# Openings that end job by job, gates that open by halves, and a gate chain woven into the splits of a ten-stage float32 kernel

## The chip, the cores and the metric

The kernel runs on one core of a Trainium2 chip. The metric is the device time in microseconds of one execution; lower is better. The engines are called PE (TensorE), DVE (VectorE, "the vector engine"), ACT (ScalarE), POOL (GpSimd) and SP (SyncE, which here only issues DMAs). Each engine runs its own list of instructions in order and they meet in semaphores.

## The reference, cut to what matters

One sequence of 512 positions and 1024 features goes through two blocks in float32. The first has four layers (a gated convolution, "fox" attention with forget gates, a gated delta rule "gdn", and sliding window attention "swa"), each as x = x + mixer(rms_norm(x)). The second has two layers, each a mixer ("hg", then latent attention "mla"), a squared-relu MLP and a gated embedding ("ple"), with a norm behind each:

```python
for i in range(2):
    a = rms_norm_2(h, pre_mix_norm[i])
    m = hgrn2_mixer(a, ...) if i % 2 == 0 else mla_mixer(a, positions, ...)
    h = h + rms_norm_2(m, post_mix_norm[i])
    f = squared_relu_mlp(rms_norm_2(h, pre_mlp_norm[i]), w_mlp_in[i], w_mlp_out[i])
    h = h + rms_norm_2(f, post_mlp_norm[i])
    e = p[i] @ w_ple_proj[i]
    g = sigmoid(h @ w_ple_gate[i])
    h = h + rms_norm_2(g * e, ple_norm[i])
```

In the fox layer a small projection gives one forget logit a head: log_f = log_sigmoid(f_logit + b_f), c = cumsum(log_f), and the scores get c_i - c_j. In mla the rotary part of queries and key is turned by cos and sin of positions times inverse frequencies.

## The kernel before, in words

All activations are kept transposed: 8 tiles of 128 features by 512 positions. Everything that is multiplied is split into a high part (rounded to the fast float32 format, fp32r) and a low part (the rest), and each product is three matmuls: high x high, low x high, high x low (L1269 to L1271; L421 to L423 for the products of `product`). The work of PE is a list of **jobs**. A job is one block of weights, 8 tiles of 128 x 128 for 128 output features, and so 24 matmuls into one PSUM bank. Jobs go through four slots (`SLOTS`) in turn: slot, bank and buffers are the job's number modulo 4. SP loads the raw weights of a job (L284), ACT writes their high part (`weight_high`, L355, 128 x 1024, for the job three or four ahead, and only when the job that had the slot is done), POOL writes the low part in two halves (L371), PE waits for the first half at the job's start and for the second at its fifth tile (`job_parts`). ACT's `weight_high` calls are written by hand between its other work, so POOL's work and PE's jobs hang on ACT's order.

Activations are split the same way: ACT writes the high part, DVE the low part, and PE waits tile by tile (`split_wait`).

**Statistics.** For an rms norm the squares of the 8 tiles are added up in `root` by DVE (L545, L755). PE multiplies the sum with a matrix of ones (L489 in `stat_tensor`, L627 in `stat_sum`), ACT takes Ln and Exp (L504, L506, `root_scalar`) and so gets `rstd`. `preload_act_table_set` makes ACT load its function table at that place (ACT_TABLE_LOAD); other loads are put in by the compiler where a function of another set follows.

`stat_tensor` stands at the end of hg, ple0, mla and ple1. It puts three matmuls of the identity with a matrix of ones (`keep_busy`, L478, float32, result unused) before the statistics matmul and eight behind it.

**Raw openings.** After the norm the next stage starts on unscaled activations. `raw_quad` runs the first four jobs of mlp0, mlp1, mla and of both ple gates together, tile by tile: for each of tiles 0 to 6 three matmuls of each of the four jobs, then the last tile of each job; in mlp and mla the statistics matmul comes after the second of these. In mlp the norm's `rstd` is applied behind the job (L2777 on DVE: relu and scale), then ACT squares (L2738) and copies (L2740), and only then comes the `weight_high` of job 4, which PE needs next. `raw_opening` does the like for fox, gdn, swa and hg.

**ple.** `ple_pe` first runs two projection jobs (their slots are those of gate jobs 2 and 3), then `raw_quad` over gate jobs 0 to 3, then jobs 4 to 7. `ple_act` takes out the projections, splits (`post_act`), and issues `weight_high` for gate jobs 2 and 3 after its steps k = 3 and k = 6 of 8. Then for each gate job n it waits for the job, issues the `weight_high` of job n + 4, takes the sigmoid out of the bank (L2892) and squares the product of the job before. In ple0 it also issues the DMA of the positions before this loop, and `rope_sines` (L1931, L1932) after job 5. `ple_dve` multiplies gate and embedding (L2919), adds squares, and in ple0 does two steps of `rope_angles` (L1904 to L1917, 15 instructions, each waiting for the one before) after each gate product.

**fox.** `raw_opening` runs jobs fox_f (gate logits) and c0 (q of head 0), `opening` jobs c0+1 and c0+2 (k and v) as the normed splits fox_h arrive, then PE waits for the copy of v, transposes it (L1040) and goes into head 0. ACT does all eight splits, then Exp and Ln of the gate chain (L1088, L1090), three weight copies, and then the loop over heads (L1097: copies of q, k, v). DVE does all of `renorm_vector`, then the gate chain (L1133 to L1148), one after the other.

**mla.** Five input jobs and a key job, norms of the query and key latents (`mla_q`, `mla_kv`), then four rope jobs, each giving two products (bank of the job, and one bank "second" that all four share, claimed anew by each). ACT copies both out (L3127, L3129), PE multiplies each with the rotation matrix (L3009), DVE turns it (L3219, L3220, L3222). ACT does the whole kv norm before the first of these copies. Then come the head pairs; their first scores are L3067.

## Time and profile before

| what | before |
|---|---|
| median of 3 runs | 2883.2 us (2882.43 to 2883.86) |
| profiled execution | 2881.76 us, span 2879.9 us |
| PE busy | 2720.0 us (94%) |
| DVE, ACT, POOL busy | 48%, 42%, 37% |
| matmuls | 13740 |
| mean granted clock of PE | 0.984 |

Times in rows are microseconds from the start of the span. PE's matmuls are pipelined: a 128 x 512 matmul is recorded as 0.39 us and the next starts 0.23 us after it, so the distance of starts is what counts. A granted clock of 1.00 is 2.4 GHz, of 0.50 is 1.2 GHz.

### The profile page before, as it was taken

To read this page: it belongs to the slowest core of one execution; us is meant where nothing else is said; L and a number is where in the kernel's file an instruction comes from. 1 tells how busy PE (TensorE), PEld (TensorE's weight loads), DVE (VectorE), ACT (ScalarE), POOL (GpSimd) and SP (SyncE) were. 2 spreads that over 40 slices of the span, in tenths; PEclk is the share of its full clock that TensorE was granted. 3 is DMA by queue.
4 is the path that set the end of the run, shared out by engine and by line. 5 is a ranking of instruction groups with operands and counts; after the bars stand their busy time and mean duration, and the time that the engine had idled before them with its cause. 6 is when DMAs were issued, how large, how long until landed. Compare 5 with 4: busy or idle time off the path is not lost.

```text
span 2879.9 us, 41743 instructions
## 1 busy us (share of the span) xinstructions
PE 2720.0 (94%) x13740; PEld 2142.4 (74%) x13740; DVE 1384.1 (48%) x2462; ACT 1212.5 (42%) x1881; POOL 1072.0 (37%) x803
## 2 busy tenths in 40 slices
PE   7999999899999899999999999988899999999997
PEld 6887777667676677778887888876667767788875
DVE  6335333776767567577655112246653444222134
ACT  4224433544443545465544233334453453333242
POOL 5454333422322332344343444433412213444442
PEclk9999999999999999999999999999999999999999
DMA  4322222211111221222222333321201102333331
GB/s 165 95 88 83 70 73 66 74 52 44 46 41 48 61 74 59 74 73 75 71 81 62 107 98 99 99 80 59 81 30 49 53 29 66 93 97 94 95 95 44
DMA packets 59639, 211.84 MB, mean 74 GB/s; under 512 B 6688, under 2 KB 7072, under 8 KB 59552
## 3 DMA queue, kind: packets, MB, share of 16 engines
q1 hardware_dynamic: 57744, 206.89, 23.4%
q10 hardware_dynamic: 1520, 2.75, 0.3%
q8 instruction: 53, 0.87, 0.1%
q0 software_dynamic: 288, 1.05, 0.1%
q14 instruction: 34, 0.28, 0.0%
HBM read 208.57 MB, written 2.10 MB: 73 GB/s over the span
## 4 chain that ended last, share of the span: by engine, by line
issue 46%; PE 24%; POOL 22%; DVE 7%; ACT 1%; POOLq 0%; DMA 0%; DVEq 0%; SPq 0%; ACTq 0%
POOL weights_low L371 22%; PE bank L1269 7%; PE bank L1271 6%; PE bank L1270 6%; DVE work L1705 2%; PE bank L1372 1%; PE bank L1050 1%; PE bank L1070 1%; DVE work L1702 0%; DVE work L954 0%; DVE work L952 0%; PE bank L1354 0%; PE bank L1059 0%; DVE activations_low L451 0%; DMA weights_raw<-weights 0%
## 5 line engine op out<-in xcount | busy, mean ns | idle before, releaser
L371 POOL TENSOR_TENSOR weights_low<-weights_raw,weights_high 128x512 fp32r<-128x512 f32 x776 | 1043.2, 1367 | 1659.0 <-ACT weights_high L355 1641.3
L1269 PE MATMUL bank<-activations_high,weights_high 128*128 128x512 f32 x2912 | 1189.9, 409 | 57.4 <-POOL weights_low L371 39.8
L1271 PE MATMUL bank<-activations_high,weights_low 128*128 128x512 f32 x2912 | 1144.2, 393 | 0.0
L1270 PE MATMUL bank<-activations_low,weights_high 128*128 128x512 f32 x2912 | 1142.9, 392 | 0.0
L1269 PEld LDWEIGHTS bank<-activations_high,weights_high 128*128 128x128 f32 x2912 | 552.4, 190 | 195.7 <-POOL weights_low L371 40.3
L1271 PEld LDWEIGHTS bank<-activations_high,weights_low 128*128 128x128 f32 x2912 | 551.0, 189 | 117.8
L1270 PEld LDWEIGHTS bank<-activations_low,weights_high 128*128 128x128 f32 x2912 | 553.1, 190 | 111.6 <-issue 9.6
L355 ACT ACTIVATE weights_high<-weights_raw 128x1024 fp32r<-128x1024 f32 x384 | 403.7, 1053 | 336.6 <-PE bank L1271 329.4
L2791 DVE TENSOR_TENSOR mixed<-bank,mixed 128x512 f32 (+1 forms) x48 | 33.2, 692 | 193.9 <-PE bank L1271 193.9
L2777 DVE SCALAR_TENSOR_TENSOR work<-bank,rstd 128x512 f32<-128x512 f32 x64 | 44.2, 691 | 158.9 <-PE bank L1271 144.2
L2738 ACT ACTIVATE to_split<-work 128x512 f32<-128x512 f32 x64 | 40.5, 632 | 189.4 <-DVE work L2777 189.4
L2782 DVE TENSOR_TENSOR activations_low<-to_split,activations_high 128x512 f32 x64 | 46.1, 721 | 104.5 <-ACT activations_high L2740 104.5
L1705 DVE SCALAR_TENSOR_TENSOR work<-work 128x512 f32<-128x512 f32 x72 | 81.0, 1125 | 2.0
L421 PE MATMUL bank<-activations_high,weights_high 128*128 128x512 f32 x168 | 73.2, 436 | 8.6 <-DVE activations_low L451 3.0
L1372 PEld LDWEIGHTS bank<-work 64*64 64x64 f32 x1344 | 47.7, 134 | 38.6 <-issue 38.6
L423 PE MATMUL bank<-activations_high,weights_low 128*128 128x512 f32 x168 | 66.8, 397 | 0.0
L1372 PE MATMUL bank<-work 64*64 64x64 f32 x1344 | 58.3, 223 | 8.8 <-DVE work L1813 7.8
L422 PE MATMUL bank<-activations_low,weights_high 128*128 128x512 f32 x168 | 66.5, 396 | 0.0
L3261 DVE TENSOR_REDUCE sink_rows<-bank 128x1 f32<-128x512 f32 x64 | 44.1, 688 | 34.7 <-PE bank L3071 34.7
L755 DVE TENSOR_TENSOR root<-root,squares 128x512 f32<-128x512 f32 x48 | 42.9, 895 | 35.4 <-ACT squares L746 34.9
L1590 ACT ACTIVATE work<-bank 128x256 f32<-128x256 f32 x40 | 15.5, 387 | 104.2 <-PE bank L1372 104.2
L3091 PE MATMUL bank<-work 128*128 128x512 f32 x128 | 56.8, 597 | 1.3 <-ACT work L3169 1.3
(438 smaller groups left out, 3151.2 us busy)
## 6 DMA issues: line engine op xcount, KB each, us to landing
weights_raw<-weights SPq DMA_DIRECT2D x388, 512.0 KB, 3.6
out_t<-residual SPq DMA_DIRECT2D x8, 256.0 KB, 2.0
residual<-x_t ACTq DMA_DIRECT2D x2, 512.0 KB, 7.6
residual<-x_t POOLq DMA_DIRECT2D x2, 512.0 KB, 10.0
work<-p_t ACTq DMA_DIRECT2D x2, 512.0 KB, 4.7
const<-consts SPq DMA_DIRECT2D x1, 713.0 KB, 12.7
const<-consts SPq DMA_DIRECT2D x1, 321.0 KB, 11.6
root<-positions ACTq DMA_DIRECT2D x1, 256.0 KB, 3.1
```

What stands on the lines that cost most here:

```text
L355: e.K.nc.scalar.activation(e.K.w_hi[:, s, :], e.K.raw[:, s, :], ACT.Copy).then_inc(js["high"], 1)
L371: K.nc.gpsimd.tensor_tensor(K.w_lo[:, s, part], K.raw[:, s, part], K.w_hi[:, s, part].bitcast(F32), ALU.subtract).then_inc(K.job_sems["low ...
L421: K.nc.tensor.matmul(dst, wh, K.act_hi[:, t, :], start=first, stop=False)
L422: K.nc.tensor.matmul(dst, wh, K.act_lo[:, t, :], start=False, stop=False)
L423: ins = K.nc.tensor.matmul(dst, wl, K.act_hi[:, t, :], start=False, stop=last)
L1269: K.nc.tensor.matmul(dst, wh, K.act_hi[:, t, :], start=k == 0, stop=False)
L1270: K.nc.tensor.matmul(dst, wh, K.act_lo[:, t, :], start=False, stop=False)
L1271: ins = K.nc.tensor.matmul(dst, wl, K.act_hi[:, t, :], start=False, stop=k == len(tiles) - 1)
L1372: ins = mm(chunk(bank(use)[h, :], c), lhs[h, c, :], rhs[h, c, :], start=True, stop=True)
L1705: ins = v.scalar_tensor_tensor(t, u[:, n:n + S], b.taps[:, 4 * part + n:4 * part + n + 1], t, ALU.mult, ALU.add)
L2782: v.tensor_tensor(at(K.act_lo, n + DT), K.y[:, 0, :], at(K.act_hi, n + DT).bitcast(F32), ALU.subtract).then_inc(K.sem("split_done"), 1)
L3091: ins = mm(dst[:, :], b.v_tok[h][:, t, :], b.pt[h][:, t, :], start=t == 0, stop=t == QT - 1)
```

## The change

It edits eight places. (1) `stat_tensor` puts five identity matmuls behind the statistics matmul where it had eight. (2) `raw_quad` goes over the four jobs together for six tiles (`EARLY`), then ends each job with its last two tiles, one after the other, and the statistics matmul comes after the first of them. (3) The ple gates open with a new `quad_by_halves`: four tiles of each of the four jobs in turn, then the other four tiles of each. (4) In fox the gate chain is done between the splits on ACT and DVE, the weight copies are spread, and head 0 is written out ahead of the loop. (5) In hg and mla the table is preloaded before the output projection, and `root_scalar` comes before the next weight copy. (6) The positions are fetched in mlp0, and ple0 computes angles and sines before its first gate product. (7) In ple the weight copies of gate jobs 2 and 3 come one step earlier, and table load and root come behind the last square and before the next weight copy. (8) In mla the first pair of rope products is copied out before the kv norm, and each pair is rotated before the next job's second product.

```diff
-        keep_busy(e, 8)
+        keep_busy(e, 5)
...
 def raw_quad(e, c, split, stage=None, tiles=A_TILES):
     jobs = [job_parts(e, c + r, None, tiles) for r in range(4)]
-    for k in range(DT - 1):
+    for k in range(EARLY):
         split_wait(e, split, k + 1)
         for parts in jobs:
             next(parts)
-    split_wait(e, split, DT)
     for r, parts in enumerate(jobs):
-        next(parts)
-        if stage and r == 1:
+        for k in range(EARLY, DT):
+            split_wait(e, split, k + 1)
+            next(parts)
+        if stage and r == 0:
             stat_sum(e, stage)
+
+def quad_by_halves(e, c, split, tiles):
+    jobs = [job_parts(e, c + r, None, tiles) for r in range(4)]
+    for half in (range(DT // 2), range(DT // 2, DT)):
+        for parts in jobs:
+            for k in half:
+                split_wait(e, split, k + 1)
+                next(parts)
...
 def fox_act(e):
-    renorm_scalar(e, "fox", cf)
-    e.eng.wait_ge(K.sem("tables_in"), 32)
     st = e.steps
+    weight_high(e, cf + AHEAD)
+    root_scalar(e, "fox")
+    h = norm_split_parts(e, "fox_h", DT)
+    take(h, 5)
     e.eng.wait_ge(K.sem("fox_x"), 1)
     st.step(nc.scalar.activation(b.e[0:H8, :], b.e[0:H8, :], ACT.Exp))
+    take(h, 1)
     st.wait()
     nc.scalar.activation(b.e[0:H8, :], b.e[0:H8, :], ACT.Ln, bias=K.c("ones")[0:H8, 0:1]).then_inc(K.sem("fox_ln"), 1)
-    for r in range(3):
-        weight_high(e, c0 + r + AHEAD)
-
-    def head(i, more):
+    take(h, DT)
+    e.eng.wait_ge(K.sem("tables_in"), 32)
+    weight_high(e, c0 + AHEAD)
+
+    def head(i, more, first=False):
         for r in range(3):
             job_wait(e, c0 + r, i)
             nc.scalar.activation(...)
+            if first and r == 0:
+                weight_high(e, c0 + 1 + AHEAD)
+        if first:
+            weight_high(e, c0 + 2 + AHEAD)
...
-    with e.eng.Fori(0, H8 - 1) as i:
-        head(i, True)
+    head(0, True, True)
+    with e.eng.Fori(0, H8 - 2) as n:
+        head(n + 1, True)
...
 def fox_dve(e):
-    take(renorm_vector(e, "fox", cf), 2 * DT)
     e.eng.wait_ge(K.sem("tables_in"), 32)
-    job_wait(e, cf)
+    renorm = renorm_vector(e, "fox", cf)
+    st.step(v.memset(b.rows.bitcast(F32), 0.0))
     (three settings of the mask)
+    take(renorm, 5)
+    job_wait(e, cf)
     st.step(v.tensor_scalar(x, bank_of(e, cf)[0:H8, :], K.col("fox_b_f", 0)[0:H8, :], None, ALU.add))
...
     v.scalar_tensor_tensor(ee, x, -1.0, x, ALU.mult, ALU.min).then_inc(K.sem("fox_x"), 1)
+    take(renorm, 1)
     e.eng.wait_ge(K.sem("fox_x"), 1)
     st.step(v.tensor_scalar(x, x, 0.0, None, ALU.min))
+    take(renorm, 1)
+    e.eng.wait_ge(K.sem("fox_ln"), 1)
     st.wait()
-    e.eng.wait_ge(K.sem("fox_ln"), 1)
     st.step(v.tensor_tensor(x, ee, x, ALU.subtract))
     st.wait()
     st.step(v.tensor_tensor_scan(ncum, K.c("ones")[0:H8, :], x, 0.0, ALU.mult, ALU.add))
-    st.step(v.memset(b.rows.bitcast(F32), 0.0))
+    take(renorm, DT)
...
 (hg_act; mla_act likewise, for its second output projection)
+    nc.scalar.preload_act_table_set("natural_log_exp_and_others")
     ahead_act(e, "hg_out")
+    root_scalar(e, "hg_post", False)
     weight_high(e, FIRST_JOB["mlp0"] + AHEAD)
-    root_scalar(e, "hg_post")
...
 def mlp_act(e, name, layer):
+    if layer == 0:
+        fetch_positions(e, K.positions_2, ROPES_BEFORE, mla_angles(K)[2])
...
 def ple_pe(e, name):
-    raw_quad(e, gate, name + "_h", None, B_TILES)
+    quad_by_halves(e, gate, name + "_h", B_TILES)
...
 def ple_act(e, name, layer):
-        if k in (3, 6):
-            weight_high(e, gate + 2 + k // 6)
+        if k in (2, 5):
+            weight_high(e, gate + 2 + k // 5)
...
     if not nth:
-        fetch_positions(e, K.positions_2, ROPES_BEFORE, mla_angles(K)[2])
+        rope_sines(e, *mla_angles(K)[:2], ROPES_BEFORE)
     for n in range(DT):
...
-        if n == 5 and not nth:
-            rope_sines(e, *mla_angles(K)[:2], ROPES_BEFORE)
+    square(DT - 1)
     K.nc.scalar.preload_act_table_set("natural_log_exp_and_others")
-    square(DT - 1)
+    root_scalar(e, name + "_post", False)
     if gate + DT + AHEAD < N_JOBS:
         weight_high(e, gate + DT + AHEAD)
-    root_scalar(e, name + "_post", False)
...
 def ple_dve(e, name, layer):
     if not nth:
-        e.eng.sem_inc(K.sem("position_room"), 1)
         cos, sin, ints, ang, turns = mla_angles(K)
-        angles = rope_angles(e, "mla_freq", cos, sin, ROPES_BEFORE, ints.bitcast(I32), ang, turns)
+        take(rope_angles(e, "mla_freq", cos, sin, ROPES_BEFORE, ints.bitcast(I32), ang, turns), 8)
     for n in range(DT):
...
-        take(angles, 2)
...
 def mla_pe(e):
     for k in range(1, 4):
         first(k)
         done(k - 1)
+        turn(k - 1)
         second_of(k)
-        turn(k - 1)
...
 def mla_act(e):
-    root_scalar(e, "mla_kv", False)
-    norm_split_scalar(e, "mla_ckv", 2, DT + 3)
     for k in range(4):
-        job_wait(e, c0 + k)
+        second.wait("second", k)
         act(mla_turned(b, 2 * k), ...)
-        second.wait("second", k)
         second.read("second", act(mla_turned(b, 2 * k + 1), ...))
+        if k == 0:
+            root_scalar(e, "mla_kv", False)
+            norm_split_scalar(e, "mla_ckv", 2, DT + 3)
```

## Rows read from the trace of the kernel before

**Rows 1.** Waits of PE: line, released by: us in total, times, longest
```profile
PE bank L1269 <- POOL weights_low L371: 39.8, 9, 9.6
PE bank L1040 <- ACT work L1097: 11.7, 8, 5.7
PE bank L489 <- DVE root L545: 8.5, 2, 7.2
```

**Rows 2.** Stretches: length; busy us (instructions) PE, PEld, DVE, ACT, POOL; clock, DMA
```profile
1600.00:1700.00 100.00, 100.00 (x443) 82.80 (x442) 18.69 (x27) 29.70 (x36) 48.12 (x38) 1.00 0.31 96
1577.40:1583.20 5.80, 5.73 (x14) 4.49 (x15) 3.15 (x4) 4.10 (x6) 4.94 (x5) 0.50 0.39 101
1250.50:1256.00 5.50, 5.47 (x65) 4.78 (x66) 4.66 (x10) 2.53 (x3) 3.82 (x3) 1.00 0.53 150
2034.00:2040.00 6.00, 5.99 (x19) 4.78 (x20) 1.85 (x3) 1.22 (x2) 2.51 (x2) 0.73 0.20 53
```

**Rows 3.** Timeline, entry of fox: start, duration, instruction [idle before, releaser]
```profile
264.48 2.93 ACT L355 ACTIVATE weights_high<-weights_raw 128x1024 fp32r<-128x1024 f32 x3
267.43 1.28 ACT L1097 ACT_TABLE_LOAD   x1
268.72 1.58 ACT L1097 ACTIVATE work<-bank 128x512 f32<-128x512 f32 x3
270.54 1.09 PE L1040 MATMUL bank<-const,work 128*128 128x128 f32 x4 [5.70 <-ACT work L1097]
...
302.68 0.63 PE L1040 MATMUL bank<-const,work 128*128 128x128 f32 x4 [0.87 <-ACT work L1097]
...
332.34 0.63 PE L1040 MATMUL bank<-const,work 128*128 128x128 f32 x4 [0.87 <-ACT work L1097]
```

**Rows 4.** Timeline, from the end of hg into mlp0
```profile
1539.69 2.74 PE L478 MATMUL bank<-const 128*128 128x512 f32 x6
1542.37 1.28 ACT L513 ACT_TABLE_LOAD   x1
1547.39 0.75 DVE L2294 SCALAR_TENSOR_TENSOR activations_low<-residual,param,activations_high 128x512 fp32r<-128x512 f32 x1
1549.61 0.79 PE L1269 MATMUL bank<-activations_high,weights_high 128*128 128x512 f32 x1
...
1565.12 0.69 DVE L545 TENSOR_TENSOR root<-root,squares 128x512 f32<-128x512 f32 x1
1570.47 1.02 PE L627 MATMUL bank<-root,const 128*128 128x512 f32 x2
...
1577.47 0.80 PE L1269 MATMUL bank<-activations_high,weights_high 128*128 128x512 f32 x1 [4.61 <-POOL weights_low L371]
```

**Rows 5.** Timeline, gates of ple0 and the statistics behind them
```profile
1928.97 3.11 POOL L371 TENSOR_TENSOR weights_low<-weights_raw,weights_high 128x512 fp32r<-128x512 f32 x2 [4.83 <-ACT weights_high L355]
1930.44 0.80 PE L1269 MATMUL bank<-activations_high,weights_high 128*128 128x512 f32 x1 [6.98 <-POOL weights_low L371]
...
1953.72 0.47 PE L1269 MATMUL bank<-activations_high,weights_high 128*128 128x512 f32 x1 [1.20 <-ACT mixed L2892]
...
1985.52 2.08 PE L489 MATMUL bank<-root,const 128*128 128x512 f32 x2 [7.19 <-DVE root L545]
```

**Rows 6.** Line L1909 (angles in swa, then in ple0): ns min/median/max, starts, form
```profile
L1909 DVE CAST root<-to_split x2: 427/427/427, 930.4 to 935.3; 128x512 int32<-128x512 f32 x2
L1909 DVE CAST work<-work x2: 1396/1399/1402, 1959.2 to 1967.6; 128x512 int32<-128x512 f32 x2
```

**Rows 7.** Timeline, mla: the first rope product and the first score
```profile
2034.01 0.79 PE L421 MATMUL bank<-activations_high,weights_high 128*128 128x512 f32 x1 [2.97 <-DVE activations_low L451]
...
2080.70 0.40 PE L3067 MATMUL bank<-const_rounded,to_split_rounded 128*128 128x512 f32 x1
```

**Rows 8.** Timeline, gates of ple1
```profile
2837.80 0.47 PE L1269 MATMUL bank<-activations_high,weights_high 128*128 128x512 f32 x1 [1.20 <-ACT mixed L2892]
...
2861.01 1.28 ACT L2897 ACT_TABLE_LOAD   x1
```

More of the change, by code:

```diff
@@ L2771, in mlp_dve @@
         Ring(e, "ple_aux", (4, 5, 6), PLE_USES).begin()
+        e.eng.sem_inc(K.sem("position_room"), 1)
     stat_vector(e, name)
@@ L2910, in ple_dve @@
     e.eng.sem_inc(K.sem("y_done"), DT + 2)
-    angles = iter(())
     if not nth:
-        e.eng.sem_inc(K.sem("position_room"), 1)
         cos, sin, ints, ang, turns = mla_angles(K)
-        angles = rope_angles(e, "mla_freq", cos, sin, ROPES_BEFORE, ints.bitcast(I32), ang, turns)
+        take(rope_angles(e, "mla_freq", cos, sin, ROPES_BEFORE, ints.bitcast(I32), ang, turns), 8)
     for n in range(DT):
@@ L3174, in mla_act @@
                             .then_inc(K.sem("split_high_done"), 1)
+        if part:
+            K.nc.scalar.preload_act_table_set("natural_log_exp_and_others")
         ahead_act(e, out)
+    root_scalar(e, "mla_post", False)
     weight_high(e, FIRST_JOB["mlp1"] + AHEAD)
-    root_scalar(e, "mla_post")
     take(post_act(e, "mla", "mlp1_h", 0, mlp_col(K, 1), "mlp1"), DT)
```

## The prediction, made before the changed kernel was built or run

> **What bounds the kernel now.** I read the waits of PE first, then the granted clock by stretch, then the order of instructions at each seam that the change touches. PE is busy 94% of the span, so little is to be won inside the long projection loops; what is left are waits between stages, and they are few and long. Nine waits of L1269 (the first product of a weight tile) for the POOL split L371 sum to 39.8 us, two waits of the statistics matmul L489 for the vector sum to 8.5 us, eight of the fox transposes for ScalarE to 11.7 us [rows 1]. The second thing to see is that a wait is paid twice. In a long undisturbed stretch 443 matmuls go in 100 us, 0.226 us each, at granted clock 1.00 (2.4 GHz); behind the 4.6 us wait at 1577 the clock is 0.50 (1.2 GHz) for 5.8 us and 13 to 14 matmuls take 0.43 us each, 2.7 us lost [rows 2]. Behind a 3.5 us wait at 1247 it stayed at 1.00, behind one of 3.0 us at 2031 it fell to 0.73 for 6 us [rows 2]. So at each long wait I count the wait and, apart from it, the matmuls that the trace shows at 1.2 GHz behind it. Everything from one seam to the next is bound by PE with no wait left in it, so what a seam gives comes off the end in full.
>
> Below, times are the profiled execution's. A product of one 128-row tile is three matmuls, 0.68 us; a job is eight, 5.44 us.
>
> **Fox entry.** Before, ScalarE does all eight splits of fox_h, then Exp and Ln, then three weight copies in a row (2.93 us), then a table load (1.28 us) and the copies of q, k and v; PE starts at 270.54 after 5.70 us idle [rows 3]. After, one weight copy stands before the q copy and one before the k copy, and because head 0 is written out ahead of the loop the Copy there follows Exp/Ln and needs no table load. Against that the gate chain now sits among the splits: in my step-through splits 6 and 7 come near 264.4 and 265.2, PE finishes jobs c0+1 and c0+2 near 267.1 instead of 264.8, and the v copy ends near 268.0, so the transposes start at 268.3: 2.3 us earlier, with the idle time cut in pieces of about 1.9 and 1.1 us. Head 0 takes 32.14 us, the next head 29.66 [rows 3]: that 2.5 us is mainly the low clock behind the wait; I count 1.7 of it. Term 4.0 us; bounds 0 (the woven chain delays the splits by all it saves) to 5.7 (the whole wait goes).
>
> **Entry of mlp0, and of mlp1, which repeats it.** Three changes. (1) Three identity matmuls fewer after the sum. Three cost 2.57 us (six records, two to a matmul, 2.74 us with the tail of the last) [rows 4]. The first split is ready at 1548.14, PE starts only when the identities end, effectively 1550.0 (row 1549.61, whose first instruction is long). (2) The table load stands ahead of the output projection, so Ln follows the sum directly: 0.3 us less (the load ends at 1543.65, the sum was ready at 1543.3) [rows 4]. The first product then starts at the split plus 0.4, about 1548.2: 1.8 us gained, against 2.57 removed; the split is late next. (3) raw_quad now puts the statistics matmul after 78 matmuls instead of 90: 12 x 0.2267 = 2.7 us earlier. The last addition of the squares ends at 1565.8 and moves 0.3 earlier, the matmul would come at 1566.0: it just fits [rows 4]. From the statistics matmul to job 4's first product is a chain of 7.0 us (Ln, Exp, relu, square, copy, weight copy, POOL half), 1570.47 to 1577.47, untouched [rows 4]. So job 4 starts at 1573.0, 4.5 us earlier, and PE waits 2.0 us instead of 4.6. The clock then most likely stays up; I count 1.9 of the 2.7 us. Term 6.4 us, twice (12.8); bounds 2.5 (only half of the advance, clock still falls) to 7.2 each. The weight copy put behind the root (1.04 us) ends a microsecond before the first split asks ScalarE, and its tile is read first 2 us later: nothing.
>
> **ple gates by halves (ple0, ple1).** Before, tile 0 goes over all four gate jobs at once, and the weights of the third and fourth aren't split: PE waits for both, 6.98 us for the second, and runs its first matmuls behind that at 0.43 us [rows 5]. After, jobs 0 and 1 do four tiles each first (5.4 us of work), and the two weight copies are issued one step of 1.98 us earlier. The POOL split of the fourth, at 1928.97 before [rows 5], moves to about 1927.0. Its cover: POOL's 3.11 us now falls on the split of tile 3, which PE needs at once, an estimated stall of 1.9 us. Job 3 starts at 1929.2, the quad ends at 1942.8 with clock 1.00, against about 1952.4. In ple1 nothing is between that and job 4, whose ScalarE work hangs on job 0 alone, now done 8.8 us before the quad ends instead of 2: job 4 starts 11.0 us earlier than 2837.80 [rows 8] allows now. At its end the table load of 1.28 us [rows 8] moves behind the last square and under the sum: 1.1 us. Term for ple1 12.1 us; bounds 9 to 13.5.
>
> In **ple0** the rotary angles come in between. (Their positions are fetched in mlp0 already: one issue on ScalarE's queue before a weight copy that has a 5.4 us job to hide in, nothing; SP's and POOL's queues are passed by no step.) Their fifteen vector instructions now stand together, before the gate products, and ScalarE waits for them and does the sines before it serves job 4. With POOL idle the int cast takes 0.43 us, with POOL working 1.40 [rows 6]. There POOL has nothing to do until ScalarE goes on, so eleven at 0.46 and four of two operands at 0.73 (estimates with 0.03 of gap), 8.0 us, from 1932.7 to 1940.8. Then Sin table, two sines, weight copy, Sigmoid table, one sigmoid, release: 5.6 us. Job 4 starts at 1946.4 against 1953.72 [rows 5], behind a wait of 3.6 us for which I count the full clock loss of 2.7. What this buys comes later: before, the interleaved angles and a switch Sigmoid, Sin, Sigmoid made the sum wait 7.19 us, till 1985.52 [rows 5]. After, jobs 4 to 7 end at 1970.8, sigmoid, product, square and addition take 3.0, the sum goes at 1973.8 and ends 1.0 us faster at full clock: Ln 12.7 us earlier. Before, the identities behind it run at low clock until well past the first split; after, the split is late next, 2.9 more. Term to the first product of mla 15.6 us; bounds 8 (the angles run contended, five times 1.4) to 20 (no low clock, no wait).
>
> **mla.** Statistics after job 0 free ScalarE's chain 2.2 us earlier at the start; about 1.5 of it survives to row 2034.01. From there to the first score, 2080.70, is 46.7 us [rows 7], in which PE has 114 matmuls of 0.227, nine rotations and a sum of 0.86, about 34 us. Serving the first turned pair before the kv norm takes away the 2.45 us wait for the second bank, and rotating before the second product gives the vector engine its work a product earlier, so that its chain, which ends last, no longer waits for PE; 7.0 us. Term 8.5; bounds 3 to 10.4.
>
> Sum: 4.0 + 12.8 + 12.1 + 15.6 + 8.5 = 53.0 us. The profiled execution took 2881.76 us (span 2879.9, 1.9 around it), 1.44 below the median of 2883.2. 2881.8 - 53.0 = 2828.8, and 2830.2 against the median.
>
> A table load is followed here by the next instruction at once: it starts at 267.43, lasts 1.28, and the copy starts at 268.72 [rows 3]. The Trainium skill, page "ScalarE: Activation LUTs", section "What ACT_TABLE_LOAD costs", puts a switch at about 1.28 us plus a drain of 1.38. By it the loads taken off the path would be worth 1.4 us more at five places and the two in front of ple0's job 4 cost 2.8 more: an estimate of 57 us for the sum. The trace doesn't show that drain, so I go by the row.
>
> **Rivals.** (A) The angle chain binds. Fifteen serial steps ahead of the first gate product: if POOL's work overlaps them after all, eleven at 1.40 and four at 1.76 are 23 us, job 4 of ple0 starts 14.7 us later and ple0 gives nothing: gain 38, 2845 us. For it: both speeds stand in the trace [rows 6]. Against: the next weight copy is queued behind the sines. (B) The shortened waits still drop the clock. Six places keep waits of 1 to 3 us; at 1.3 to 3 us lost in each, 12 us: 2842 us. For it: 3.0 us idle did it at 2031; against: 3.5 us at 1247 didn't [rows 2]. (C) The next waits are close behind: vector work for the last splits and POOL's second halves hold PE where I let it run, and each term is near its lower bound (0 + 5 + 9 + 8 + 3 = 25): 2858 us. (D) The other side: PE falls to 1.2 GHz and stays there over a projection phase, in the mlp entries, where the identities that kept it busy are fewer. Each matmul then costs 0.2 us more, so it decides from 265 matmuls on, 11 jobs; 500 of them would give 2930 us. For it: each long wait was followed by such a stretch; against: none lasted beyond about 10 us of the trace. That the edits don't do what they say is small: PE idles at 1572, 1923 and 1978 for just the instructions that are reordered.
>
> **Chances.** Forecast (gain 45 to 60) 0.50, A 0.12, B 0.20, C 0.12, D 0.03, no change 0.03. Predicted 2830.2 us. The range goes from 2820 (a few terms at their good ends) to 2856 (near C), which leaves out about 2 in 10. Less than 0.2% (5.8 us) can't be told from no change here. Faster by more: 0.94; within: 0.03; slower: 0.03.
>
> **What would show it.** The waits of L1269 for L371 fall from nine and 39.8 us to under 22, none of 7 us left. The wait of 7.19 us at L489 is gone. In mlp0 the statistics matmul comes after 78 products and job 4 waits about 2 us at clock 1.00. In ple0 a new wait of 3 to 4 us for the first sigmoid, behind sines that follow 8 us of unbroken angle work. Head 0 of fox has no table load before its copies. From the first product of mla_rope to the first score about 40 us. It is wrong if the clock is 0.50 behind job 4 of the mlp stages, if the angle casts take 1.40, or if fox_h's last splits hold PE longer than its transposes start earlier.

## The result, and the profile after

The changed kernel takes 2829.09 us (median of 4 runs, 2827.98 to 2830.99), the kernel before 2882.81 beside it (2881.93 to 2883.86): ratio 0.9817, 95% interval 0.9804 to 0.9829, 53.7 us. The forecast was 2830.2. The profiled span is 2827.4 us against 2879.9.

The waits of PE in the changed kernel (line waited at, releasing line: us in all, times, longest), which answer to [rows 1]. L1269 is now L1292, L1040 is L1051, L1097 is L1112, L2294 is L2317, L2892 is L2919:
```profile
PE bank L1292 <- POOL weights_low L371: 17.2, 5, 9.5
PE bank L1292 <- DVE activations_low L451: 7.8, 9, 1.5
PE bank L1051 <- ACT work L1112: 6.9, 8, 0.9
PE bank L1292 <- DVE activations_low L2317: 6.1, 3, 2.1
PE bank L1292 <- ACT mixed L2919: 2.1, 1, 2.1
PE bank L421 <- DVEq L3247: 2.0, 1, 2.0
PE bank L489 <- DVE root L545: 0.5, 2, 0.2
```
The long waits between the stages are gone: both of 7 us at the gates, the 7.2 us at L489, the 5.7 us of the transposes, and 4.6 us became 1.9. The 9.5 us that are left are the start of the kernel, where nothing was changed (9.6 before). Two lines are new and were not forecast as such: three waits of 2.0 us for L2317, the first split of mlp0, mla and mlp1, and one for the key rotation (L3247). The waits for L451, low parts of activations too, rose from 3.7 us (6 times) to 7.8 (9 times).

The timeline after, same columns as [rows 3 to 5]; fox, mlp0's entry, ple0:
```profile
263.34 1.04 ACT L355 ACTIVATE weights_high<-weights_raw 128x1024 fp32r<-128x1024 f32 x1
264.29 0.58 ACT L1112 ACTIVATE work<-bank 128x512 f32<-128x512 f32 x1
267.37 0.63 PE L1051 MATMUL bank<-const,work 128*128 128x128 f32 x4 [0.88 <-ACT work L1112]
297.01 0.63 PE L1051 MATMUL bank<-const,work 128*128 128x128 f32 x4 [0.87 <-ACT work L1112]
...
1537.87 1.04 ACT L355 ACTIVATE weights_high<-weights_raw 128x1024 fp32r<-128x1024 f32 x1
1538.99 3.36 POOL L371 TENSOR_TENSOR weights_low<-weights_raw,weights_high 128x512 fp32r<-128x512 f32 x2 [5.98 <-ACT weights_high L355]
1539.47 1.77 DVE L2322 SCALAR_TENSOR_TENSOR mixed<-mixed,param,rstd 128x512 f32<-128x512 f32 x1
1541.16 1.75 DVE L2317 SCALAR_TENSOR_TENSOR activations_low<-residual,param,activations_high 128x512 fp32r<-128x512 f32 x1
1542.96 0.50 PE L1292 MATMUL bank<-activations_high,weights_high 128*128 128x512 f32 x1 [2.08 <-DVE activations_low L2317]
1560.83 1.02 PE L627 MATMUL bank<-root,const 128*128 128x512 f32 x2
1567.84 0.50 PE L1292 MATMUL bank<-activations_high,weights_high 128*128 128x512 f32 x1 [1.89 <-POOL weights_low L371]
...
1919.67 1.28 ACT L1954 ACT_TABLE_LOAD   x1
1920.29 0.42 DVE L1927 CAST work<-work 128x512 f32<-128x512 int32 x1
1928.38 0.63 ACT L1954 ACTIVATE work<-work 128x512 f32<-128x512 f32 x1 [7.43 <-DVEq L1942]
1930.50 1.28 ACT L2919 ACT_TABLE_LOAD   x1
1931.79 0.60 ACT L2919 ACTIVATE mixed<-bank 128x512 f32<-128x512 f32 x1
1932.53 0.47 PE L1292 MATMUL bank<-activations_high,weights_high 128*128 128x512 f32 x1 [2.07 <-ACT mixed L2919]
1957.36 1.13 PE L489 MATMUL bank<-root,const 128*128 128x512 f32 x2 [0.23 <-DVE root L545]
```
No table load stands before fox's copies, and head 0 takes 29.64 us. In mlp0 the weight copy behind the root wakes POOL at 1538.99, and the vector engine's two instructions beside it take 1.77 and 1.75 us; the first split took 0.75 before [rows 4]. In ple0 the angle work stands in one piece, from 1920.29 to the first sine at 1928.38, and the sum waits 0.23 us instead of 7.19.

The cut by stage, from the starts of the sum matmuls (L627, L489) and the first score, gains in us. "Again" is a second profiled execution of the same program (experiment 11):
```
stage                         before   after   again   gained  forecast
fox entry and heads           294.43  288.77  288.84     5.7      4.0
next two stages (gdn, swa)    672.24  671.19  671.60     1.0      0
hg                            330.84  330.85  330.84     0        0
mlp0                          367.18  361.57  361.56     5.6      6.4
ple0, to its own sum           76.08   60.26   60.28    15.8     11.7
mla, sum to first score        95.18   87.20   85.65     8.0     12.4
mla, the rest                 345.70  345.55  345.51     0.1      0
mlp1                          367.17  363.17  361.54     4.0      6.4
ple1, to its own sum           70.14   57.95   57.97    12.2     12.1
```
Ahead of the first line and behind the last nothing changed, so this is the 52.5 us of the span (forecast 53.0). The forecast's 15.6 for ple0 splits here into 11.7 up to the start of its sum matmul and 3.9 behind that start, 1.0 of it the sum itself; the 3.9 stand in mla's line.

The granted clock, of before, after and again (span, mean clock):
```profile
core 0: 2879.9 us, clock 0.984
```
```profile
core 0: 2827.4 us, clock 0.991
```
```profile
core 0: 2826.3 us, clock 0.993
```
0.016 of 2879.9 us is 46 us of matmul time lost to the lower level, 0.009 of 2827.4 is 25, 0.007 is 20. So at most 21 to 26 us of the gain is clock, and less in fact, since PE loses nothing where it idles at the low level; the rest is time in which PE no longer waits.

### The profile page after: what moved, and what is told of

Same layout as the page of the kernel before. It is cut to its first block, busy times and chain, and to the rows that moved or that the text cites. A ratio compares the mean times of both kernels' runs of the same rounds, so it can differ in the third digit from the quotient of the medians.

```text
span 2827.4 us, 41684 instructions
## 1 busy us (share of the span) xinstructions
PE 2694.7 (95%) x13716; PEld 2128.3 (75%) x13716; DVE 1397.5 (49%) x2462; ACT 1209.3 (43%) x1879; POOL 1075.5 (38%) x803
## 4 chain that ended last, share of the span: by engine, by line
issue 38%; PE 36%; POOL 17%; DVE 7%; ACT 1%; DMA 0%; POOLq 0%; DVEq 0%; SPq 0%; ACTq 0%
POOL weights_low L371 17%; PE bank L1292 11%; PE bank L1294 10%; PE bank L1293 10%; DVE work L1728 1%; PE bank L1395 1%; PE bank L1061 1%; PE bank L1081 1%; DVE activations_low L451 1%; PE bank L1377 0%; DVE work L1725 0%; DVE work L965 0%; DVE work L963 0%; DVE to_split L676 0%; PE bank L1070 0%
## 5 line engine op out<-in xcount | busy, mean ns | idle before, releaser
L1292 PE MATMUL bank<-activations_high,weights_high 128*128 128x512 f32 x2912 | 1185.3, 407 | 44.7 <-POOL weights_low L371 17.2
L1292 PEld LDWEIGHTS bank<-activations_high,weights_high 128*128 128x128 f32 x2912 | 550.1, 189 | 183.0 <-issue 20.7
L1395 PE MATMUL bank<-work 64*64 64x64 f32 x1344 | 58.3, 223 | 8.8 <-DVE work L1836 7.8
L1613 ACT ACTIVATE work<-bank 128x256 f32<-128x256 f32 x40 | 15.4, 385 | 104.2 <-PE bank L1395 104.2
```

Of the source, the lines that this page charges most:

```text
L1292: K.nc.tensor.matmul(dst, wh, K.act_hi[:, t, :], start=k == 0, stop=False)
L1395: ins = mm(chunk(bank(use)[h, :], c), lhs[h, c, :], rhs[h, c, :], start=True, stop=True)
```

## The experiments

The 95% intervals of the medians below reach some 4.7 us to either side, and the time to the second sum alone, ahead of every edit, went from 244.5 to 246.9 us between executions. A difference under some 5 us between two medians is therefore not told from nothing; what a smaller one consists of is read from the stages of the profiled execution, cut as above. Differences are to the changed kernel's 2829.1 us.

**1. The old quad.** `raw_quad` as before: seven tiles over four jobs, statistics behind the second.
```diff
-    for k in range(EARLY):
+    for k in range(DT - 1):
...
-        if stage and r == 0:
+        if stage and r == 1:
```


> The changed kernel with the opening quad of mlp0, mlp1 and mla as it was (seven tiles over all four jobs, statistics matmul behind the second job, after 90 products instead of 78). Theory (the order of the quad carries the mlp terms): job 4 of mlp0 and mlp1 waits 4.6 us again instead of 1.9, and runs its first matmuls at clock 0.50, 4.6 us each, and 1 us more at the entry of mla: 9 to 11 us slower than the changed kernel, about 2839 us. Rival (the shorter identity run and the early table load made the mlp gain, 9.8 us in the two stages together): under 3 us slower, 2829 to 2832.


Measured 2844.5 us, 15.4 more. The waits of L1292 for POOL rise from 17.2 to 23.7 us, job 4 of mlp0 waits 4.6 us, and behind it the clock is at 1.2 GHz. The stretch from 1574.50 (length; busy us and count of PE, PEld, DVE, ACT, POOL; clock, DMA), then the changed kernel's from 1567.80:
```profile
1574.50:1580.50 6.00, 5.48 (x13) 4.33 (x14) 3.14 (x4) 4.28 (x7) 5.14 (x5) 0.50 0.35 93
```
```profile
1567.80:1573.60 5.80, 5.76 (x25) 4.80 (x26) 3.17 (x4) 4.09 (x6) 4.96 (x4) 1.00 0.42 110
```
mlp0 is 368.5 us long against 361.6 (and 367.2 before), mlp1 366.9 against 363.2, mla to its first score 89.3 against 87.2. These three make 12.7 of the 17.3 us between the two profiled spans. The edit doesn't touch the other 4.6: 1.5 ahead of the second sum, and low-clock stretches of 1.5 in hg (332.4) and 1.6 in ple0 (61.9). The theory stands, the rival falls: without the order of the quad mlp0 would be no shorter than before. The price of 4.6 us for each mlp stage was 2.3 too low in mlp0, where a second low-clock stretch stood behind the first product, and 0.9 too high in mlp1, where the changed kernel's first execution had such a stretch itself.

**2. No halves.** The ple gates tile by tile over four jobs, their copies behind tiles 4 and 7.
```diff
-    quad_by_halves(e, gate, name + "_h", B_TILES)
+    quad_old(e, gate, name + "_h", None, B_TILES)
...
-        if k in (2, 5):
+        if k in (3, 6):
```


> The changed kernel with the ple gates opened as before (tile by tile over four jobs, weight copies behind tiles 4 and 7). Theory: in ple1 11 us come back; in ple0 the quad ends near 1940.2 instead of 1930.5 and job 4 starts 1.2 us behind it, 8.9 us later than now, so 20 us slower in all, about 2849 us, with the 7 us wait for the fourth job's weights back in both. Rival (in ple0 the rotary angles set job 4 whatever the order of the gates, and only ple1 pays): 11 to 12 us slower, about 2841 us.


Measured 2849.4 us, 20.4 more. ple0 to its sum 68.5 us (+8.3), ple1 68.8 (+10.9), and the wait is back:
```profile
1920.82 0.80 PE L1306 MATMUL bank<-activations_high,weights_high 128*128 128x512 f32 x1 [6.95 <-POOL weights_low L371]
1943.49 0.47 PE L1306 MATMUL bank<-activations_high,weights_high 128*128 128x512 f32 x1 [1.19 <-ACT mixed L2933]
```
As the theory said, to 1 us; the rival, that ple0's part would stay, falls.

**3. The angles in the loop.** Positions, angle instructions and sines of ple0 where they were, the halves kept.
```diff
-        rope_sines(e, *mla_angles(K)[:2], ROPES_BEFORE)
     for n in range(DT):
...
+        if n == 5 and not nth:
+            rope_sines(e, *mla_angles(K)[:2], ROPES_BEFORE)
...
+        take(angles, 2)
```


> The changed kernel with the rotary angles of ple0 as before: positions fetched in ple0, two angle instructions behind each gate product, sines behind the sixth sigmoid. Theory (the moved angles freed the statistics of ple0): job 4 starts 2.1 us earlier without the wait for the first sigmoid, the sum matmul waits 7 us again and the identities behind it run at low clock (1.9 us): 6.8 us slower, about 2836 us. Rival (the halves made all of the gain of ple0 and the angles only added the 2.07 us wait): 0 to 2 us faster than the changed kernel, 2827 to 2829 us.


Measured 2829.9 us, the same as the changed kernel (+0.8, not told from nothing). The theory falls, and the rival, that the halves made all of ple0's gain, is the nearer one. Casts take 1.40 us again and a sum waits, but 1.9 us, not 7.2, while job 4 doesn't wait:
```profile
1930.92 1.40 DVE L1932 CAST work<-work 128x512 int32<-128x512 f32 x1
1947.41 1.28 ACT L1954 ACT_TABLE_LOAD   x1
1956.62 1.13 PE L489 MATMUL bank<-root,const 128*128 128x512 f32 x2 [1.90 <-DVE root L545]
```
With experiment 2 the square is full. ple0 to its own sum:
```
                      angles in the loop    angles ahead of the gates
tile by tile               76.1 (before)         68.5 (exp. 2)
by halves                  59.6 (exp. 3)         60.3 (after)
```
Moving the angles is worth up to 7.6 us alone and nothing beside the halves. It is "up to", because the runs other than "before" also have the table load behind the last square: in ple1, which has no angles, experiment 2 is 1.3 us shorter than the kernel before (68.8 against 70.1), and as much of the 7.6 can be the load's, which has no experiment of its own. The two edits hide the same work: with halves job 0 is done 8 us before the quad ends, and the interleaved angles fit into that. That they fit is read from the trace of experiment 3, not tested apart.

**4. The old order in mla.**
```diff
-        turn(k - 1)
         second_of(k)
+        turn(k - 1)
...
+    root_scalar(e, "mla_kv", False)
+    norm_split_scalar(e, "mla_ckv", 2, DT + 3)
     for k in range(4):
```


> The changed kernel with the start of mla as before (rotations behind the second product, kv norm ahead of the first turned pair). Theory: the waits of 2.45, 1.15 and 1.93 us come back for those of 1.22, 0.45 and 2.02, and the first score comes 46.7 us behind the first rope product instead of 41.2: 5.5 us slower, about 2834.6 us. Rival (the earlier start from ple0 changed what falls beside POOL's work, and the order itself is worth little): under 2 us slower.


Measured 2831.9 us, +2.8. From the first rope product to the first score:
```profile
2005.91 0.50 PE L421 MATMUL bank<-activations_high,weights_high 128*128 128x512 f32 x1 [2.29 <-DVE activations_low L451]
2016.54 0.50 PE L421 MATMUL bank<-activations_high,weights_high 128*128 128x512 f32 x1 [2.46 <-ACT work L3151]
2036.29 2.08 PE L3031 MATMUL bank<-work,const 128*128 128x512 f32 x2 [1.93 <-DVE work L3244]
2049.10 0.40 PE L3089 MATMUL bank<-const_rounded,to_split_rounded 128*128 128x512 f32 x1
```
43.2 us, against 46.7 before, 41.2 after and 39.7 in the second execution. The old waits of 2.46, 1.14 and 1.94 us are back to 0.3 us, and yet it is 3.5 us faster than before: there three stretches of 6 us in this part ran at a mean clock of 0.73, 0.72 and 0.72, here one, from 2036.00, at 0.72. The changed kernel's first execution also has one such stretch, its second none. So, like with like, 2.0 us is the order, and 3.5 us are the two low-clock stretches fewer. Neither is the size that was expected, and the median (+2.8) doesn't tell theory from rival.

**5. The weight copy in front of the root.**
```diff
-    root_scalar(e, "hg_post", False)
     weight_high(e, FIRST_JOB["mlp0"] + AHEAD)
+    root_scalar(e, "hg_post", False)
```
and the same for mla and ple.


> The changed kernel with the weight copy back in front of the root at the end of hg, mla and the ple stages, the early table load kept. Theory (contention): POOL's split of that weight tile now ends before the vector engine's first steps instead of lying beside them, where a two-operand instruction takes 1.75 us instead of 0.74; the 2.0 us waits of the first products of mlp0, mla and mlp1 go: 5 to 6 us faster than the changed kernel, about 2823.5 us. Rival (the copy holds the root up, as it did before the change): its 1.04 us stands in front of the logarithm at three entries: 0 to 3 us slower, 2829 to 2832 us.


Measured 2827.8 us (2824.1 to 2829.7), 1.3 less. The entry of mlp0:
```profile
1536.94 1.04 ACT L355 ACTIVATE weights_high<-weights_raw 128x1024 fp32r<-128x1024 f32 x1
1538.06 2.72 POOL L371 TENSOR_TENSOR weights_low<-weights_raw,weights_high 128x512 fp32r<-128x512 f32 x2 [2.68 <-ACT weights_high L355]
1542.85 0.75 DVE L2317 SCALAR_TENSOR_TENSOR activations_low<-residual,param,activations_high 128x512 fp32r<-128x512 f32 x1
1543.65 0.50 PE L1292 MATMUL bank<-activations_high,weights_high 128*128 128x512 f32 x1 [0.42 <-DVE activations_low L2317]
```
From sum to first product 5.76 us against 7.43 in mlp0, 5.62 against 7.43 in mlp1, 7.02 against 7.43 in mla. There the copy follows the table load, ends 0.3 us too late for the root, and POOL's split still lies beside a vector instruction of 1.85 us. The three gains make 3.9 us. Low-clock stretches took them back: behind the wait of job 4 in mlp0 (361.5 us long, as with the copy behind), in ple0 (61.9 against 60.3) and in mlp1, and in hg (332.4). Contention is shown as the cause of the waits in mlp0 and mlp1; in mla the wait only fell from 2.0 to 1.6 us. The gain can't be told from nothing in this run.

**6. Eight identities.** `keep_busy(e, 8)` behind the sum.


> The changed kernel with eight identity matmuls behind the sum, as before. Theory (the split is late by 2.0 us whatever PE does): the three identities, 2.6 us, fill the wait of 2.0 us, the first products come 0.5 us later at three entries, and less is run at low clock behind them: within 2 us of the changed kernel, 2828 to 2831 us. Rival (the forecast's term, 1.8 us at each entry from the shorter run): 5.4 us slower, about 2834.5 us.


Measured 2832.1 us (+3.0, not told from nothing). In the trace the first product comes 7.43 us behind the sum in mlp0, as with five; the stages agree with the second execution of the changed kernel (experiment 11) to 0.5 us but for mlp1 (363.5, with a low-clock stretch). The shorter run alone bought nothing, as the theory said. With the copy in front of the root (experiment 5) PE starts 5.76 us behind the sum, which eight identities, ending only at 7.4, would not let it do; the two were not run together.

**7. No identities.** The same call left out.


> The changed kernel with no identity matmuls behind the sum. Theory (the idle time drops the clock): PE waits 6 us at the entries of mlp0, mla and mlp1, the first product comes when it does now, and behind it the clock is 0.50 for some 6 us, 3 us lost at each: about 9 us slower, 2838 us. Rival (the clock falls at these places without regard to the wait): 0 to 2 us slower, 2829 to 2831 us.


Measured 2832.6 us, +3.5. PE waits 6.4 us and starts at clock 0.50:
```profile
1542.53 0.79 PE L1291 MATMUL bank<-activations_high,weights_high 128*128 128x512 f32 x1 [6.37 <-DVE activations_low L2316]
```
```profile
1542.50:1548.50 6.00, 5.97 (x14) 4.71 (x15) 6.00 (x11) 3.08 (x5) 0.00 (x0) 0.50 0.29 90
```
From each of the three sums to the next (28.1, 27.4 and 27.6 us) it costs 2.8, 0.6 and 0.7 us against the changed kernel's first execution, which had low clock behind its own 2 us wait at the last two, and 2.8, 0.6 and 2.3 us against its second, which had it at the middle one. Against experiment 10, which had it at none (25.3 each), it costs 2.9, 2.1 and 2.3. So 4 to 7 us, not 9: the direction right, the size too high. The median alone doesn't show even the direction clear of noise.

**8. The old fox streams.** `fox_act` and `fox_dve` as before.


> The changed kernel with the scalar and vector streams of fox as before. Theory: the transposes wait 5.7 us again, 3.2 us later than now, and head 0 runs at low clock behind them, 2.5 us: 5.6 us slower, about 2834.7 us. Rival (the stretch at low clock there comes and goes from execution to execution, and only the shorter wait belongs to the edit): 3 us slower, about 2832 us.


Measured 2836.5 us, +7.4; the fox stage is 294.5 us against 288.8 (+5.7), with this wait:
```profile
271.88 1.08 PE L1051 MATMUL bank<-const,work 128*128 128x128 f32 x4 [5.71 <-ACT work L1108]
```
The theory's number for the stage; the rest of 7.4 lies outside it. The low clock came back with the wait, and none of the twelve profiled executions with the new streams has any there, so the rival, which left it to chance, falls.

**9. Gate copies behind tiles 4 and 5.** `if k in (3, 4): weight_high(e, gate + k - 1)`.


> The changed kernel with the weight copies of the third and fourth gate job behind tiles 4 and 5 (k = 3 and 4) instead of tiles 3 and 6 (k = 2 and 5). Theory (the stall at tile 3 is POOL's split lying beside the two vector instructions that PE waits for): the 1.4 us wait at 1909.05 of ple0 and the one of ple1 go, the split falls on tiles 4 to 7 that are read some 8 us later: 2.8 us faster, 2826.3 us. Rival (the work only moves): the same stall comes at tile 4 or at the third job's weights, no change.


Measured 2829.9 us, no difference. Half and half: the 1.39 us stall becomes one of 0.52 at the last tile of job 0, ple1 gains 0.9 us (57.1), and in ple0 the angles end later and take it back in front of job 4:
```profile
1923.26 0.50 PE L1292 MATMUL bank<-activations_high,weights_high 128*128 128x512 f32 x1 [0.52 <-DVE activations_low L451]
1935.37 0.47 PE L1292 MATMUL bank<-activations_high,weights_high 128*128 128x512 f32 x1 [2.93 <-ACT mixed L2919]
```

**10. Sines behind the third sigmoid.** The angles stay ahead of the gate products.
```diff
-        rope_sines(e, *mla_angles(K)[:2], ROPES_BEFORE)
...
+        if n == 2 and not nth:
+            rope_sines(e, *mla_angles(K)[:2], ROPES_BEFORE)
```


> The changed kernel with the angles where they are (unbroken, ahead of the gate products), but the sines behind the third sigmoid instead of ahead of the first. Theory: the weight copy and the sigmoid that job 4 waits for run at 1922 to 1925, while the vector engine works on the angles; the 2.07 us wait at 1930.47 goes: 2 us faster, 2827.0 us. Rival (contention): POOL's split of job 5's weights now lies beside the angle chain, where a cast takes 1.40 us instead of 0.43; angles, gate products and squares come some 10 us late, and the sum waits as in the kernel before: 3 to 7 us slower.


Measured 2826.9 us, 2.2 less, which by the medians alone is not told from nothing; the stage shows it, ple0 58.1 us (-2.2), with no wait of job 4. The contention is there, and has room:
```profile
1923.92 3.05 POOL L371 TENSOR_TENSOR weights_low<-weights_raw,weights_high 128x512 fp32r<-128x512 f32 x2 [5.77 <-ACT weights_high L355]
1927.30 1.40 DVE L1932 CAST work<-work 128x512 int32<-128x512 f32 x1
1955.49 1.13 PE L489 MATMUL bank<-root,const 128*128 128x512 f32 x2 [0.32 <-DVE root L545]
```

**11. The changed kernel again.**


> The changed kernel once more, beside the others on one chip. Theory (the low-clock stretches are partly chance): the instructions' order and the waits of PE are the same to 0.1 us, but low-clock stretches come at other places than in the first profile, and the stages differ by up to 2 us; the median is 2829, within 2 us. Rival (the clock follows the waits alone): the same stretches at the same places.


Measured 2829.7 us (2826.8 to 2833.2). The waits of the changed seams are within 0.03 us of the first execution's, and mla is 1.6, mlp1 1.6 us shorter (the table), because no low-clock stretch stood behind the first rope product and mlp1's first product. Here are the 6 us behind mlp1's first product, which waits 2.01 us in the first execution and 2.00 in the second; clock is the third number from the end:
```profile
2397.54:2403.54 6.00, 6.00 (x19) 4.78 (x20) 6.00 (x11) 3.11 (x5) 0.00 (x0) 0.72 0.31 87
```
```profile
2398.05:2404.05 6.00, 6.00 (x26) 4.98 (x27) 6.00 (x11) 3.13 (x6) 0.00 (x0) 1.00 0.26 87
```
The rival falls: equal waits don't give equal clocks.

**12. Experiments 5, 9 and 10 together.**


> The changed kernel with three edits together: the weight copy in front of the root, the gate copies behind tiles 4 and 5, the sines behind the third sigmoid. Theory (they touch different waits, so their gains in the traces add): 1.7, 1.8 and 0.4 us at the three first products, 0.9 us in each ple stage, 2.2 us at job 4 of ple0, 7.9 us in all: about 2821 us. Rival (the clock takes it back): as with the weight copy alone, low-clock stretches appear behind the 1.9 us waits of job 4 once the waits before them are gone, and half is lost: 2825 us or more.


Measured 2820.2 us (2819.4 to 2822.9), ratio to the kernel before 0.9782, interval 0.9769 to 0.9796, which lies below the changed kernel's 0.9804 to 0.9829: 8.9 us less. Of its waits:
```profile
PE bank L1292 <- DVE activations_low L451: 6.0, 9, 1.5
PE bank L1292 <- DVE activations_low L2317: 2.2, 3, 1.6
PE bank L489 <- DVE root L545: 1.7, 2, 1.4
```
mlp1 359.8 us, ple0 58.3, ple1 57.1, and mla to its first score 83.8. A sum waits 1.4 us now where job 4 waited 2.1. The theory's 7.9 us holds by the median. The rival is seen in the profiled execution, but small: mlp0 (361.5) gained nothing, with low clock behind job 4, and hg lost 1.6. This version beats both kernels.

## Why the forecast was right, and where it was not

The time came within 1.1 us, by a sum whose terms were off by up to 4.4 us each way. What was edited did remove the waits that it was to remove, so the mechanism held in the main; that the total was off by so little is luck, since ple0 and fox gave 5.8 us more than was forecast and mla and the mlp stages 7.6 less.

- **Fox**, 4.0 forecast, 5.7 shown (experiment 8). Both halves of the step were too small: the transposes started 3.2 us earlier, not 2.3, and head 0 became 2.5 us shorter, not the 1.7 that I counted.
- **mlp entries**, 6.4 each, 5.6 and 4.0 (5.6 in the second execution). The statistics matmul twelve products earlier is the term: the wait behind it is 1.89 us at clock 1.00, as forecast, and it carries the stage (experiment 1). But in mlp0 it comes 25.3 us behind hg's sum where it came 28.2 us behind it, 2.9 earlier and not 4.5. The 1.8 us of the shorter identity run are missing (0.2 are there), and 2.7 us of low clock went instead of the 1.9 that I counted. The step that failed is "the weight copy put behind the root ... nothing". I looked at who reads the copied tile, not at what POOL's split of it lies beside: two of the vector engine's first steps take 1.77 and 1.75 us, so the first split is ready 7.4 us behind the sum, where it was ready 5.9 us behind it before, and the three identities taken away are worth nothing (experiments 5, 6).
- **ple1**, 12.1 forecast, 12.2. The stall of the split at tile 3, the fourth, was put at 1.9 and is 1.4.
- **ple0**, 11.7 to the start of its sum, 15.8. The angles start where they were forecast, 23.2 us behind mlp0's last sum matmul (1920.29 here; the forecast's 1932.7 is 23.3 behind it in the old trace), and take the 8.0 us. The step that failed is the next one, 5.6 us with the Sin table in it: that table was loaded at 1919.67, while ACT waited, so job 4 comes 1.5 us earlier and waits 2.07 us, not 3.6. Behind it the clock stays at 1.00, where I had counted a full loss of 2.7 us. The two make the 4.1 us. The second is partly luck: of the nine profiled executions that have this wait (2.0 to 2.9 us) seven keep the clock; experiments 1 and 5 drop to 0.72, and their ple0 is 61.9 us. And the cause was misnamed: "the interleaved angles" made the sum wait 7.19 us only together with the late gates; the halves alone cut that to 1.9 us (experiments 2, 3).
- **mla**, 12.4 with what came from ple0's sum, 8.0 (9.5 in the second execution). From the sum to the first rope product it gained 2.5 us (48.5 to 46.0), where 5.4 were forecast: the first product still waits 2.0 us for its split (experiment 5 gave back 0.4 of it here). From there to the first score it gained 5.5 us (7.0 in the second execution), where 7.0 were forecast. Of these some 2.0 are the order's and the rest is low clock of the kernel before (experiment 4), and there is a new wait of 2.0 us for the key rotation. So the size came near, but not by the reason given.
- The 1.0 us of gdn and swa, where nothing was changed, is a shorter low-clock stretch (7.0 us of it before, 3.6 after). It belongs to no edit and was not forecast.

Rival A (contended angles, 2845) fell: the casts took 0.43 us. Where they did take 1.40 (experiments 3, 10) ple0 was no longer either (59.6 and 58.1 us against 60.3). B held in small: behind the waits of 2.0 and 2.3 us at 1964.79 and 2003.35 the first execution of the changed kernel still shows this:
```profile
1965.00:1971.00 6.00, 6.00 (x20) 4.77 (x20) 6.00 (x11) 3.32 (x6) 0.00 (x0) 0.72 0.29 90
2003.40:2009.40 6.00, 6.00 (x19) 4.71 (x20) 1.79 (x3) 1.32 (x3) 2.51 (x2) 0.74 0.16 38
```
That is 6 us with 20 and 19 matmuls instead of 26 to 27, some 1.5 us each. C (every term near its lower bound, 2858) fell. The vector work that it named shows in the waits for L451, 4.1 us more than before, three of them 1.3 to 1.4 us long (fox, both ple gates), which the terms had counted at 1.9. The three 2.0 us waits are for first splits, which no rival named. D needs a fall that lasts; with all identities gone (experiment 7) it lasted some 10 us, 4 of them while PE idled, and cost 2.9.

Behind the Sigmoid load (1930.50 and 1.28) the sigmoid starts at 1931.79. The drain that the Trainium skill gives, page "ScalarE: Activation LUTs", section "What ACT_TABLE_LOAD costs", isn't seen here, and the 57 us by it came out further off than the sum by the rows.

## What to carry to other kernels

Two edits that hide the same work don't add: before summing their terms, ask of the second what is still late once the first is in. When a copy on one engine wakes a split on another, price what that split lies beside, not only who reads the tile. And count low-clock time as a term with its own spread (here 3.2 us in mla and mlp1 between two executions of one program), which a single execution can't settle.

## What was not expected of the hardware

- The same program with the same waits ran with mean clock 0.991 and 0.993, and single stages differed by 1.6 us for it.
- A table load goes ahead of the wait of the instruction that needs it: loaded at 1919.67, sine at 1928.38 after 7.43 us of waiting.
- Why some waits of 2 us have a stretch at 1.2 GHz behind them in one execution and not in the next stays open. It is not the same everywhere: behind the first products of mlp0 and mlp1 (waits of 2.08 and 2.01 us) the clock fell in 2 of 9 profiled executions each, behind that of mla (2.01 us) in 7 of 9.
